# PSUM banks of two outer products and the waits around the last level of a 64x64 block inversion, in a hybrid decoder step on one core

## What is computed

```python
l = GDN_CHUNK                                  # 64
kb = kc * bc[..., None]
a_mat = jnp.where(strict, jnp.einsum('bhnid,bhnjd->bhnij', kb, kc) * dmat, 0.0)
rhs = jnp.concatenate([vc * bc[..., None], kb * jnp.exp(gc)[..., None]], axis=-1)
sol = lax.linalg.triangular_solve(a_mat + jnp.eye(l, dtype=jnp.float32), rhs,
                                  left_side=True, lower=True, unit_diagonal=True)
def step(s, inp):                              # over the four chunks
    q_i, qk_i, u_i, w_i, k_i, gl = inp
    v_new = u_i - jnp.einsum('bhck,bhkv->bhcv', w_i, s)
    o = jnp.einsum('bhck,bhkv->bhcv', q_i, s) + jnp.einsum('bhij,bhjv->bhiv', qk_i, v_new)
    s = s * gl[..., None, None] + jnp.einsum('bhck,bhcv->bhkv', k_i, v_new)
    return s, o
```

## Time and profile before

| what | value |
|---|---|
| median of three runs | 1770.22 us |
| the profiled execution's own time | 1770.22 us |
| its span in the trace | 1768.5 us |
| granted PE clock, mean | 0.985 |
| PE matmul busy | 1689.7 us (96%) |
| DVE busy | 973.6 us (55%) |
| ACT busy | 798.9 us (45%) |
| POOL busy | 241.4 us (14%) |

### The profile page before, as it was taken

The page is one execution under the profiler, slowest core; times in us unless marked ns, Lnnn a source line. Parts: engine busy times, 40 slices in busy tenths (PEclk is TensorE's granted clock), DMA queues, the critical chain, the costliest instruction groups (busy, mean ns, idle before and its releaser), DMA issues.

```text
span 1768.5 us, 39431 instructions
## 1 busy us (share of the span) xinstructions
PE 1689.7 (96%) x17307; PEld 1566.2 (89%) x17307; DVE 973.6 (55%) x1608; ACT 798.9 (45%) x1478; POOL 241.4 (14%) x295
## 2 busy tenths in 40 slices
PE   7999999999899999989999999999999999899997
PEld 5998789999796999987876987899998998799997
DVE  6865547744556477444351354477438836357643
ACT  4755336633544365333412213465336644356533
POOL 5006230000011100020032220100010024210001
PEclk9999999999999999999989999999999999999999
DMA  7841346556653556544323000555547522255550
GB/s 202 265 149 32 85 140 190 181 180 187 191 155 122 188 172 201 178 129 128 119 86 102 21 3 9 147 189 191 184 157 226 180 73 69 67 183 183 191 167 25
DMA packets 244542, 249.68 MB, mean 141 GB/s; under 512 B 15792, under 2 KB 238350, under 8 KB 244286
## 3 DMA queue, kind: packets, MB, share of 16 engines
q1 hardware_dynamic: 236736, 223.66, 40.3%
q0 software_dynamic: 7328, 23.42, 4.5%
q10 hardware_dynamic: 308, 0.10, 0.0%
HBM read 229.23 MB, written 18.32 MB: 140 GB/s over the span
## 4 chain that ended last, share of the span: by engine, by line
PE 89%; DVE 6%; ACT 3%; issue 1%; DMA 1%; POOL 1%; DVEq 0%; POOLq 0%; ACTq 0%
PE ps L690 87%; PE ps L694 2%; DVE tri L2169 1%; DVE hn L2177 1%; DMA acts<-in_state_gdn_conv_dram 1%; DVE acts L2177 1%; ACT acts L1664 1%; DVE acts L2169 0%; ACT L1667 0%; DVE hn L2169 0%; ACT rows L1664 0%; DVE st L2169 0%; DVE w_gdn L2169 0%; POOL tri L3059 0%; ACT rstd L1664 0%
## 5 line engine op out<-in xcount | busy, mean ns | idle before, releaser
L2169 DVE TENSOR_TENSOR w_mlp<-ring,w_mlp 128x1024 fp32r<-128x1024 f32 x256 | 311.3, 1224 | 162.2 <-ACT w_mlp L1664 156.1
L1664 ACT ACTIVATE w_mlp<-ring 128x1024 fp32r<-128x1024 f32 x256 | 268.9, 1053 | 248.6 <-PE ps L690 221.0
L690 PE MATMUL ps<-hn_split,w_mlp 128*128 128x264 f32 x3072 | 374.1, 284 | 0.0
L690 PEld LDWEIGHTS ps<-hn_split,w_mlp 128*128 128x128 f32 x3072 | 372.3, 188 | 0.5
L690 PE MATMUL ps<-h_split,w_mlp 128*128 128x264 f32 x3072 | 371.8, 283 | 0.0
L690 PEld LDWEIGHTS ps<-h_split,w_mlp 128*128 128x128 f32 x3072 | 371.5, 188 | 0.0
L690 PE MATMUL ps<-acts,ring 128*128 128x264 f32 (+2 forms) x960 | 225.5, 398 | 2.9 <-DVE acts L2177 2.9
L690 PEld LDWEIGHTS ps<-acts,ring 128*128 128x128 f32 (+2 forms) x960 | 184.3, 193 | 41.0 <-issue 3.5
L690 PE MATMUL ps<-gdn_hi,w_gdn 128*128 128x264 f32 x1024 | 190.8, 286 | 8.2 <-DVE w_gdn L2169 5.9
L1664 ACT ACTIVATE tri<-ps 128x264 f32<-128x264 f32 (+4 forms) x186 | 81.7, 441 | 227.6 <-PE ps L690 221.5
L1664 ACT ACTIVATE acts<-ps 128x264 f32<-128x264 f32 (+5 forms) x140 | 63.5, 465 | 239.5 <-PE ps L690 228.7
(11 more groups left out here) (358 smaller groups left out, 1925.4 us busy)
## 6 DMA issues: line engine op xcount, KB each, us to landing
ring<-in_ffn_w_dram SPq DMA_DIRECT2D x128, 1024.0 KB, 5.2
ring<-in_gdn_w_in_dram SPq DMA_DIRECT2D x32, 1024.0 KB, 5.8
ring<-in_ml_w_in_dram SPq DMA_DIRECT2D x12, 1024.0 KB, 5.4
ring<-in_rw_w_rkv_dram SPq DMA_DIRECT2D x12, 1024.0 KB, 4.9
st<-in_state_gdn_S_dram POOLq DMA_DIRECT2D x2, 4096.0 KB, 22.3
ring<-in_gdn_w_out_dram SPq DMA_DIRECT2D x8, 1024.0 KB, 5.3
out_gdn_S_s_dram<-st SPq DMA_DIRECT2D x16, 512.0 KB, 3.9
st<-in_state_mlstm_C_dram POOLq DMA_DIRECT2D x1, 4096.0 KB, 18.9
```

The lines of the kernel that those rows point to most:

```text
L690: return nc.tensor.matmul(out, lhsT, rhs, start=start, stop=stop)
L1664: return nc.scalar.activation(out, in_, f, bias=bias, scale=scale)
L2169: return nc.vector.tensor_tensor(out, in0, in1, op)
```

## The change

Four things are edited.

1. The outer products number 3, 4 and 5 get other banks. Number 3 had (6, 3) and gets (6, 7), number 4 had (7, 2) and gets (2, 3), number 5 had (6, 3) and gets (6, 7).
2. DVE adds number 4 at place (5,1) and not at (5,2).
3. In the last level of `invert64`, PE's Q products of half h wait for bank 2+h too, which they don't write, and the table then holds both banks as read by DVE's subtraction.
4. `invert64` ends with a wait for both halves of the last level. Before, it waited for the first half, and its callers for the second: in GDN behind `solve_values(0)`, in RWKV-7 at once.

```diff
-        OUTER = ((0, (2, 1), 3, 5), (4, (3, 1), 3, 5), (1, (4, 1), 3, 5), (5, (5, 0), 6, 3), (2, (5, 2), 7, 2), (6, (5, 3), 6, 3),
+        OUTER = ((0, (2, 1), 3, 5), (4, (3, 1), 3, 5), (1, (4, 1), 3, 5), (5, (5, 0), 6, 7), (2, (5, 1), 2, 3), (6, (5, 3), 6, 7),
                  (3, None, 4, 5), (7, None, 2, 3))
...
                         b, bt = 2 + h, 4 + h
-                        if l < LEVELS64 - 1:
-                            pe.wait_ge(*last_read[b])
+                        pe.wait_ge(*last_read[b])
                         pe.wait_ge(*last_read[bt])
...
                         last.then_inc(Q_mm, count.up(Q_mm))
-                        last_read[bt] = Q_ev, count.expect(Q_ev)
-                        if l < LEVELS64 - 1:
-                            last_read[b] = last_read[bt]
+                        last_read[b] = Q_ev, count.expect(Q_ev)
+                        last_read[bt] = Q_ev, count.expect(Q_ev, 0)
...
-                pe.wait_ge(Q_ev, count.seen(Q_ev))
+                pe.wait_ge(Q_ev, count.seen(Q_ev, 2))
...
                 solve_values(0)
-                pe.wait_ge(Q_ev, count.seen(Q_ev))
                 outer_products(6)
```

## The result

The changed kernel took 1787.26 us (median of 7 runs, 1780.09 to 1792.60), the kernel before on the same chip 1772.75 us (7 runs, 1768.55 to 1777.33). The medians differ by 14.5 us, and the changed kernel's lies outside the predicted range. The profiled execution took 1789.02 us for a span of 1787.3 us, against a span of 1768.5 us before.

What follows compares the result with a forecast made beforehand. PE was taken as the bound, running with DVE as two full rows in the last inversion level. Two GDN layers at 2.54 us, RWKV-7 at 0, sum to 5.1 us: 1775.3 us, range 1771.4 to 1778.6.

Steps and rivals of the forecast that it cites:

- (a) to (d): Last inversion level: PE late 1.19 (number 3), 0.66 (first Q half), 0.93 us (`solve_values(0)`); 0.24 us back at number 7.
- the 5.1 by the row: Cost of both GDN layers if PE loads weights only once each new wait is over: 5.1 us.
- the 4.0 by the rule: Cost of both GDN layers if each new wait hides a weight load of 0.18 us: 4.0 us.
- (e): Behind `solve_keys`, everything in each GDN layer moves by the same 2.54 us.
- The clock falls in the new waits: Rival, GDN layers: gaps lower PE's clock, 1.6 us a fall; one fall 1776.9 us, two 1778.5 us; chance 0.20.
- The prediction's own sign of being wrong: Among the signs named: the clock row behind `solve_keys` changes.
- the end with two falls: The clock falling twice in the GDN layers: +8.3 us, 1778.5 us; said to be left out of the range.
- Only the last wait counts: Rival: bank waits are hidden, only the wait before `solve_values(0)` costs, 0.7 us a layer: +1.4, 1771.6 us; chance 0.12.
- not slower: Rival, last level: second half of the inverse comes earlier, PE gains 0.24 us a layer: -0.5, 1769.7 us; chance 0.06.
- DVE's wait for the state copy: Behind DVE's additions in the GDN layer: idle time that stays 2.2 to 2.5 us.

Runs made afterwards that it cites:

- e7_pause_here: The kernel before, with PE stopped three times a GDN layer at the places of the new waits until POOL finished small memsets: 1792.11 us, ratio 1.0117.
- e4_outer_only: The kernel before with only the new banks of the outer products and number 4 added at (5,1): 1775.43 us, ratio 1.0029.
- e5_fill_a: The changed kernel with four constant matmuls filling only the first new wait, before number 3's second half: 1780.38 us, ratio 1.0051.
- e2_no_bank_wait: The changed kernel without the last level's wait of the Q products for banks 2 and 3: 1790.58 us, ratio 1.0113.
- e9_fill_late: The changed kernel with six constant matmuls at the last of the three new waits only, before `solve_values(0)`: 1784.66 us, ratio 1.0077.
- e8_pause_there: The kernel before, with PE stopped three times a GDN layer for POOL memsets, between tiles of the layer's input projection: 1781.93 us, ratio 1.0059.

## Why the prediction was wrong

**The waits (a) to (d) were right.** In the layer that kept its clock, number 3 to the P half took 2.14 us against 0.94 before: +1.20, forecast 1.19. From the P half to the first Q half 2.46 against 1.74: +0.72, forecast 0.66. From there to `solve_values(0)` 3.68 against 2.72: +0.96, forecast 0.93. From `solve_values(0)` to `solve_keys` 2.13 against 2.63: -0.50, forecast -0.24; numbers 6 and 7 now run as one piece, which gains twice the 0.24 us of idle time that went. The sum is 2.38 a layer for 2.54. The first Q half to `solve_keys` is 5.81 (forecast 6.0, before 5.35), the second P half to `solve_keys` 8.27 (8.4, before 7.09). With the waits filled the kernel was 4.8 us slower where 5.1 were forecast. The weight load of number 3's second half starts with its matmul at 191.98 and not ahead of it. Two layers at 2.38 make 4.76 us, nearer to the 5.1 by the row than to the 4.0 by the rule of the Trainium skill, TensorE: Matmul & The Clock Gate, section "Architectural detail: the array is 16× 32×32, not 1× 128×128".

**The step that failed** is (e), that everything behind the waits moves by the same 2.54 us, so that the forecast has no term for the clock, and with it the price and the chance of the rival *The clock falls in the new waits*. That rival is what happened. I gave it 0.20 and 1.6 us a fall, the difference between 5.68 and 4.08 us of the same 64 records. But that was a short fall: behind `solve_keys` at 1503.62 and over by 1508, at a mean clock of 0.59 in those 4 us, so some 3 us at half speed. In the changed kernel the fall comes ahead of the first Q half and lasts 17 us in the first layer and 20 in the second, with `solve_values`, `solve_keys` and all behind them in it: 7.1 us in the first layer. In the second the profile shows 73.92 - 65.47 = 8.45 for a fall where the kernel before already paid 64.71 - 63.08 = 1.63, so 6.8 new. The difference in this pair of profiles is then 2.4 + 7.1 + 2.4 + 6.8 = 18.7 us of 18.8. That so little is left over is luck: the rest of the span differs by up to 9 us between profiles of the same kernel. The prediction's own sign of being wrong, a changed clock behind `solve_keys`, is what the profile shows. Its range wasn't what its words say either: it is said to leave out the end with two falls, but 1778.5 us, the price of two, lies inside it. With a fall at the measured price, two of them would have stood at about 1789 us.

The rows at 212 to 228 us, which I took as evidence that gaps pass at full clock, misled: they are one layer's in one execution, and three profiles of one kernel now show equal gaps with a fall and without. The same trace had a counterexample: behind the same tail of the second layer the output projection took 29.99 us instead of 28.39, at the low clock for some 3 us. The clock's mean over the recorded executions says the same: 36 of the changed kernel have 0.976 (0.970 to 0.982) and 1788.9 us, 82 of the kernel before, from the groups of runs above, 0.984 (0.980 to 0.988) and 1771.4 us. A straight line through both, with one slope, gives 1470 us per 1.0 of clock and 5.2 us between the kernels at equal clock (3.2 to 6.7 when the executions are drawn anew). Of the 17.5 us between the means, some 12 go with the clock.

What I had not weighed is another section of the page I cited: the Trainium skill, TensorE: Matmul & The Clock Gate, section "A second HAM failure mode: psum-queue depth-cycling", says that short idles between groups of matmuls, as PE goes round the PSUM banks, can make the clock go up and down. The trace agrees: no idle time of PE in the last level is above 1.23 us, and the clock falls to 0.50. That it is the banks isn't borne out: `e7_pause_here` has the old banks and falls too.

**The rest.** *Only the last wait counts* and *not slower* are refuted by the rows at 190.00 and 192.88. DVE's wait for the state copy, forecast at 2.2 to 2.5 us, is 2.20 in the layer that kept its clock and 5.95 in the one that lost it.

**Open.** Why the second GDN layer fell in three of three profiles of the changed kernel and the first in one of three; how much each single gap weighs (`e4_outer_only` has the longest gap of all and lost little, `e5_fill_a` has it filled and still scatters up to 1791); what decides how long a fall lasts (17 to 20 us in the changed kernel's profiles, 7 in `e4_outer_only` without a filler, some 3 in the kernel before, among the same kinds of matmuls); why `e2_no_bank_wait` is no faster than the changed kernel, though it has one wait fewer; and why RWKV-7's first inversion, at unchanged code, fell in two of these profiles (the second of the changed kernel and that of `e2_no_bank_wait`).

## What to carry to other kernels

A new wait of PE has two prices: its own length, which the timelines of two engines give to a tenth of a microsecond, and the chance of a low clock, which has to be priced by how long the clock may stay down in the work that follows (here up to 20 us, 7 us of time a fall) and not by the shortest fall that a trace shows. Where PE goes through small matmuls with waits between them, look at the granted clock of more than one profile before trusting it. Matmuls of a constant in waits that can't be removed cost nothing here where they stood ahead of the wait and fitted into it (a layer of 65.47 us with and without them), and cost time where they didn't fit (66.19 us with six at the last wait) or stood behind it (5.2 us). With all three waits filled the profile shows no fall at them.

## What was not expected of the hardware

- Once down, the clock stayed at 0.50 through 13 us of small matmuls without a gap (1513.70 to 1527, changed kernel), but was back behind 2.72 us of 128x128 fillers (`e9_fill_late`, 1516.65). In `e4_outer_only` it came back at about 1506.7 without fillers, in the same kind of work.
- The same three stops of PE cost 4.6 us in a layer's input projection (`e8_pause_there`) and 13.2 us in the inversion's last level (`e7_pause_here`, 76.29 us for 63.08).
- Two executions with rows equal to 0.01 us up to the Q half part there: one at 1.97 us a half, one at 1.15. The Trainium skill, TensorE: Matmul & The Clock Gate, section "Part 1: The HAM clock gate (the "warmup" mystery)", says that the moment of the change varies from run to run. Here the fall itself does.
